# Ten of sixteen key and value weight tiles of two cross attentions computed in rounds 110 to 133 of a delta recurrence

## The chip, the cores and the metric

The kernel runs on one core of one Trainium2 chip. The metric is device time in microseconds of one execution. The core has five engines that run their own instruction streams in order and meet through semaphores: TensorE (PE, matmuls and transposes), VectorE (DVE), ScalarE (ACT), GpSimd (POOL) and SyncE (SP), which here only issues DMAs.

## The reference, cut to what matters

The reference runs two transformer blocks one after the other, on 512 tokens of width 1024. The first block's first layer has a gated delta recurrence, run over 512 latent and 256 context tokens in chunks, forward and backward, for 8 heads. The second block has two layers, and each of them holds a cross attention to a memory of 256 rows. The memory is an input, so its keys and values depend on nothing that the program computes:

```
for l in range(2):
    ...
    mem_n = rms_norm(mem, norm_mem[l])
    x = x + memory_cross_attention(rms_norm(x, norm_cross[l]), mem_n, xa_w_q[l], xa_w_kv[l], ...)

def memory_cross_attention(h, mem_n, w_q, w_kv, w_o, q_norm, k_norm):
    q  = rms_norm((h @ w_q).reshape(B, S, 4, 256), q_norm)
    kv = (mem_n @ w_kv).reshape(B, M, 2, 4, 256)      # w_kv is 1024 x 2048
    k, v = rms_norm(kv[:, :, 0], k_norm), kv[:, :, 1]
    ...softmax(q k / 16) v, then @ w_o
```

All is float32.

## The kernel before, in words

**Products.** A large product is done with three matmuls in the faster float32r type: every operand is cut into a high part (ACT copies it) and a low part (DVE subtracts the high part from the raw value), and `mm3` adds high x high, high x low and low x high (lines 259 to 261). Weights come in tiles of 1 MB, 128 partitions by 2048 values. SP loads them in the order in which PE takes them, into two raw slots; a load waits until the tile before it in its slot has been cut. The cut parts go to two places in `rw`, and a cut waits until the tile before last has been used. `tile` cuts one tile ahead; tiles marked `pieces` are cut in quarters by `split_quarter` at chosen rounds instead.

**The recurrence.** `rounds` (line 1744) runs 24 units (2 groups of 4 heads, 12 chunk visits each). A unit starts every 5 rounds and lives some 23 rounds, so up to five are alive, and there are 138 rounds. In each round every engine does its step of each unit alive, in program order, and then what `pe_between`, `act_between`, `dve_between` and `pool_between` (from line 2189 on) put behind it: dense projections of the first block (until about round 108), the ada rows (`SIDE_ROUNDS`, until round 114), and from round 104 the tails. A tail takes one finished group and chunk, norms it, turns it, gates it with Z (loaded from HBM by POOL) and writes the high and low parts into `H5` or `mT`, from where the output projection `dn_out` reads them. `TAILS` holds the round of each. The units' matmuls are float32, of 32, 64 or 128 columns. Bank sets: units have six PSUM banks, dense parts and tails two.

**The cross attentions.** `pe_cross` (line 3740) runs the output projection of the mixer before it (four weight tiles), turns the normed memory behind the second of them, and then makes keys and values: `pe_proj_tok` for four blocks of 512 columns, each of two weight tiles, for two groups of 128 memory rows. A tile is 24 matmuls of 512 columns. Keys are normed for each head (`act_key_norm`, `dve_key_norm`, lines 3840 and 3849) during the value tiles, turned, and then the query projection follows. POOL loads the raw memory and the gains in `pool_cross_loads` (line 3676).

Of the kernel before, what the change touches and what calls it, by code (L numbers as in the profile page):

```python
# [8 lines left out]
F32 = mybir.dt.float32  # L9
# [88 lines left out]
class Kernel:  # L98


    def __init__(self, nc, ctx, I, consts, out):
        self.nc, self.ctx, self.I, self.consts, self.out = nc, ctx, I, consts, out
        self.sems, self.book, self.freed, self.banks, self.tiles = {}, {}, {}, {}, []
        self.raw, self.pieces, self.slots, self.rws = set(), set(), [], []
        self.rehearsing = True
        self.arena = ctx.enter_context(nc.sbuf_tensor("arena", [128, A_END], F32))
        self.rx = ctx.enter_context(nc.sbuf_tensor("rx", [128, 12288], F32R))
        self.rw = ctx.enter_context(nc.sbuf_tensor("rw", [128, 8192], F32R))
        self.psum = ctx.enter_context(nc.psum_tensor("psum", [128, 4096], F32))
# [8 lines left out]
        self.g_s = nc.dram_tensor("g_s", [128, 4096], F32).ap()  # L118
        self.ident = self.mem(CO + C_ID, 128)
# [371 lines left out]
def r2(ap, a):  # L491
    return ap.rearrange("p (a n) -> p a n", a=a)
# [1574 lines left out]
def z_rounds(rnd, offset):  # L2067
# [109 lines left out]

def act_tail_hi(a, K, i, hg, c):
    a.wait_ge(*K.at("dn", len(STREAM) - 1, 1))
    a.wait_ge(*K.at("tail_z", hg, c))  # L2180
    a.cp(tail_toks(K, hg, c)[0], tail_z(K, i)).then_inc(*a.sig(("o_hi", hg, c)))

# [3 lines left out]
    v.lo(tail_toks(K, hg, c), tail_z(K, i)).then_inc(*v.sig(("o_lo", hg, c)))  # L2186


def pe_between(p, K, side, ms, rnd):

    for i, hg, c in tail_rounds(rnd, 3):
        pe_tail(p, K, i, hg, c, PART_BANKS)
    if rnd < 2:
        pe_part_post(p, K, DENSE - 2 + rnd, UNIT_BANKS)
    r = part_rounds(rnd, 9)
# [18 lines left out]


def act_between(a, K, side, ms, rnd):
    for i, hg, c in tail_rounds(rnd, 4):
        act_tail_hi(a, K, i, hg, c)
    if rnd < 2:
# [9 lines left out]
        act_G_rows(a, K, 1)  # L2229
    if rnd in SIDE_ROUNDS:  # L2230
        next(side, None)
    if rnd in TILE_ROUNDS:
        ms.append(a.skip())
    for q in {2: (0,), 4: (1,), 7: (2, 3)}.get(rnd - max([t for t in TILE_ROUNDS if t <= rnd]), ()):
        a.split_quarter(ms[-1], q)
    if rnd in (119, 122):
        a.ahead()
    if rnd == 84:
        act_tail_root(a, K, 0)
# [1500 lines left out]
def pe_cross(p, K, l, otag, W, ready, turn=None):  # L3740
# [98 lines left out]

def act_key_norm(a, K, l, t):  # L3840
    kt = cross_mem(K)[2]
    for j in range(2):
        a.wait_ge(*K.at(f"xk{l}{j}", "out", t))
# [37 lines left out]
def act_cross(a, K, l, otag):  # L3881
# [38 lines left out]
def dve_cross(v, K, l, otag):  # L3920
# [12 lines left out]
        if (t, h) == (3, 0):  # L3933
            dve_mem_lo(v, K, l)

    dve_out(v, K, otag, 8, 4, between={0: keys}, after=after, begun=l)
    for j in range(2):
        v.tile()
        v.tile()
        dve_tok_out(v, K, f"xk{l}{j}", range(2), lambda t: kt[:, t, j * 512:(j + 1) * 512])  # L3940
    for j in range(2):
        v.tile()
        v.tile()
        dve_key_norm(v, K, l, j)
        dve_tok_out(v, K, f"xv{l}{j}", range(2), lambda t: v_[:, t, j * 512:(j + 1) * 512])
# [1070 lines left out]
```

## Time and profile before

| what | value |
|---|---|
| median of 3 runs | 4089.51 us (4084.01 to 4093.94) |
| span of the profiled execution | 4093.5 us, 67946 instructions |
| PE busy | 3847.9 us, 94% |
| DVE, ACT, POOL busy | 2094.8, 1657.1 and 535.3 us |
| in_xa_w_kv loads | 16 of 1024 KB, landing 5.0 us after issue |
| k_s loads on POOL between 640 and 900 us | 8 of 256 KB, landing 3.4 us after issue |

The profile is one execution. Busy times don't count waiting. PEclk is the TensorE clock that was granted, as a share of 2.4 GHz. Line numbers are those of the kernel's file, and most instructions carry the line of a small helper, so places are found by time: the recurrence ends and `dn_out` begins at 828.9 us; the keys and values of the first cross attention are made from 2608 to 2653 us, those of the second from 3533 to 3578 us. The profile names a group by its line, its operands and its shape.

### The profile page before, as it was taken

What the parts mean: (1) busy time and instruction counts of PE and PEld (TensorE: products, weight loads), DVE (VectorE), ACT (ScalarE), POOL (GpSimd) and SP (SyncE); (2) the same over time, 40 slices, a digit from 0 to 9 for tenths busy, and PEclk for the clock granted to TensorE, in tenths of its full rate; (3) what the DMA queues carried; (4) which work ended last, traced back from release to release, by engine and by line L of the source; (5) the groups of instructions that cost most, each with busy time, mean ns of one, the idle gap of its engine ahead of it and who ended that gap; (6) DMA issues with size and microseconds to landing.
All of it is one profiled execution on the core that took longest, in us unless ns stands there. A gap on an engine that the chain in (4) does not pass through costs nothing.

```text
span 4093.5 us, 67946 instructions
## 1 busy us (share of the span) xinstructions
PE 3847.9 (94%) x28458; PEld 3180.3 (78%) x28458; DVE 2094.8 (51%) x3092; ACT 1657.1 (40%) x2695; POOL 535.3 (13%) x607
## 2 busy tenths in 40 slices
PE   6999999799999999988999889999999998999999
PEld 4888777678888877767887765778887877788887
DVE  3667755652212454565225644545665337645564
ACT  4445544322112343453223446444344346544333
POOL 0033444311200000020200000000210013000210
PEclk8999999799999999999999899999999999999999
DMA  5244554322221121122232310412332221312232
GB/s 164 82 140 148 171 165 146 99 88 62 78 67 52 63 82 38 42 79 87 93 98 96 70 52 1 136 53 83 103 100 93 93 93 36 124 53 83 93 103 83
DMA packets 238474, 367.71 MB, mean 90 GB/s; under 512 B 9859, under 2 KB 146774, under 8 KB 237910
## 3 DMA queue, kind: packets, MB, share of 16 engines
q1 hardware_dynamic: 219248, 300.49, 22.4%
q0 software_dynamic: 18368, 62.70, 5.2%
q8 instruction: 224, 3.67, 0.4%
q14 instruction: 84, 0.69, 0.1%
q10 hardware_dynamic: 550, 0.17, 0.0%
HBM read 344.36 MB, written 18.96 MB: 89 GB/s over the span
## 4 chain that ended last, share of the span: by engine, by line
PE 77%; DVE 12%; ACT 7%; issue 1%; DMA 1%; ACTq 0%; DVEq 0%; SPq 0%; POOL 0%; POOLq 0%
PE psum L259 21%; PE psum L260 20%; PE psum L261 20%; PE psum L256 14%; ACT arena L389 3%; DVE arena L289 3%; PE psum L265 2%; DVE arena L299 2%; DVE rw L289 2%; ACT rw L393 2%; ACT rx L393 1%; DVE rx L383 1%; DVE arena L303 1%; ACT arena L393 1%; DMA arena<-in_ada_w 1%
## 5 line engine op out<-in xcount | busy, mean ns | idle before, releaser
L259 PE MATMUL psum<-rx,rw 128*128 128x512 f32 (+2 forms) x2864 | 1049.5, 366 | 33.3 <-DVE rw L289 19.0
L260 PE MATMUL psum<-rx,rw 128*128 128x512 f32 (+2 forms) x2864 | 1023.1, 357 | 0.0
L261 PE MATMUL psum<-rx,rw 128*128 128x512 f32 (+2 forms) x2864 | 1021.9, 357 | 0.0
L289 DVE TENSOR_TENSOR rw<-arena,rw 128x2048 fp32r<-128x2048 f32 (+3 forms) x266 | 548.6, 2062 | 822.4 <-ACT rw L393 812.6
L256 PE MATMUL psum<-arena 32*32 32x32 f32 (+8 forms) x12982 | 759.8, 246 | 83.4 <-ACT arena L393 25.5
L256 PEld LDWEIGHTS psum<-arena 32*32 32x32 f32 (+4 forms) x12982 | 584.3, 133 | 217.0 <-issue 84.7
L393 ACT ACTIVATE rw<-arena 128x2048 fp32r<-128x2048 f32 (+3 forms) x266 | 453.6, 1705 | 707.3 <-PE psum L261 691.1
L259 PE MATMUL psum<-rw,rx 128*128 128x512 f32 (+1 forms) x1816 | 699.5, 385 | 26.5 <-DVE rx L383 13.6
L260 PE MATMUL psum<-rw,rx 128*128 128x512 f32 (+1 forms) x1816 | 689.3, 380 | 0.0
L261 PE MATMUL psum<-rw,rx 128*128 128x512 f32 (+1 forms) x1816 | 688.4, 379 | 0.0
L259 PEld LDWEIGHTS psum<-rx,rw 128*128 128x128 f32 (+1 forms) x2864 | 545.3, 190 | 163.5 <-issue 36.6
L261 PEld LDWEIGHTS psum<-rx,rw 128*128 128x128 f32 (+1 forms) x2864 | 545.1, 190 | 78.7
L260 PEld LDWEIGHTS psum<-rx,rw 128*128 128x128 f32 (+1 forms) x2864 | 546.2, 191 | 77.1 <-issue 3.3
L393 ACT ACTIVATE arena<-psum 128x512 f32<-128x512 f32 (+6 forms) x657 | 301.1, 458 | 660.1 <-PE psum L256 284.0
L454 POOL TENSOR_TENSOR arena<-arena 128x512 f32<-128x512 f32 (+4 forms) x228 | 355.6, 1560 | 1229.6 <-DVE arena L299 391.8
L259 PEld LDWEIGHTS psum<-rw,rx 128*128 128x128 f32 x1816 | 345.4, 190 | 106.0 <-DVE rx L383 25.8
L299 DVE SCALAR_TENSOR_TENSOR arena<-arena 128x512 f32<-128x512 f32 (+6 forms) x583 | 405.8, 696 | 35.7 <-ACT arena L389 13.7
L389 ACT ACTIVATE arena<-arena 128x512 f32<-128x512 f32 (+10 forms) x483 | 251.1, 520 | 393.4 <-DVE arena L299 185.4
L261 PEld LDWEIGHTS psum<-rw,rx 128*128 128x128 f32 x1816 | 345.5, 190 | 64.6
L260 PEld LDWEIGHTS psum<-rw,rx 128*128 128x128 f32 x1816 | 345.9, 190 | 60.6
L289 DVE TENSOR_TENSOR arena<-arena,psum 128x512 f32<-128x512 f32 (+3 forms) x308 | 151.8, 493 | 348.9 <-PE psum L261 201.7
L265 PE MATMUL psum<-arena 128*128 128x128 f32 (+3 forms) x1188 | 185.3, 298 | 91.9 <-DVE arena L289 26.1
(73 smaller groups left out, 2113.6 us busy)
## 6 DMA issues: line engine op xcount, KB each, us to landing
arena<-in_ffn_w_up SPq DMA_DIRECT2D x66, 1024.0 KB, 5.1
arena<-in_ada_w SPq DMA_DIRECT2D x48, 1024.0 KB, 6.5
arena<-in_ffn_w_down SPq DMA_DIRECT2D x40, 1024.0 KB, 5.0
arena<-in_ffn_w_gate SPq DMA_DIRECT2D x22, 1024.0 KB, 5.3
arena<-in_dn_w_in SPq DMA_DIRECT2D x16, 1024.0 KB, 5.9
arena<-in_xa_w_kv SPq DMA_DIRECT2D x16, 1024.0 KB, 5.0
arena<-in_hgrn_w_in SPq DMA_DIRECT2D x16, 1024.0 KB, 5.4
arena<-in_da_w_in SPq DMA_DIRECT2D x12, 1024.0 KB, 5.1
```

What stands on the lines that cost most here:

```text
L256: return self.e.matmul(out, l, r, start=start, stop=stop)
L259: self.e.matmul(out, l[0], r[0], start=start, stop=False)
L260: self.e.matmul(out, l[0], r[1], start=False, stop=False)
L261: return self.e.matmul(out, l[1], r[0], start=False, stop=stop)
L265: return self.e.transpose(out, a, self.K.ident[0:k, 0:k])
L289: return self.e.tensor_tensor(out, a, b, op)
L299: return self.e.scalar_tensor_tensor(out=out, in0=a, scalar=s, in1=b, op0=op0, op1=op1)
L303: return self.e.tensor_reduce(out, a, AX.X, op)
L383: return self.e.tensor_tensor(dst[1], src, dst[0].bitcast(F32), SUB)
L389: return self.e.activation(out, a, f, **kw)
L393: return self.e.activation(out, a, ACT.Copy, **kw)
L454: return self.e.tensor_tensor(out, a, b, op)
```

## The change

The memory is loaded once in round 70 into a new tensor `more`, its row norms are made in rounds 82 to 86, and it is turned and multiplied with the gain of each layer's memory norm in rounds 108 and 109 (first layer) and 124 and 125 (second). The turned rows go to blocks 0 and 3 of `H5`. Ten weight tiles (column blocks 0, 1, 2 of the first layer, 0 and 1 of the second) are used in rounds 110 to 133: each piece has 12 matmuls in its round and 12 in the next. The results go through `more` to a new HBM tensor `kv_s`, stored by POOL. In the cross attentions POOL loads them back; the keys, all of which come this way, are normed after the third tile of the output projection; three or two fewer column blocks are left in the loop. Tails of chunks 0 and 3 write to blocks 0 and 3 of `H5`, so two of them move from rounds 119 and 122 to 131 and 133; tails take unit banks now. The two early cuts of `dn_out` weights move from rounds 119 to 123 to rounds 134 to 137. The SBUF for `more` (12.4 KB of each partition) is taken from the scratch for descriptors of POOL's DMAs, set to 4096 bytes. An entry of `KV_PIECES` is a round, a layer, a column block, a half of the rows of the weights and a raw slot; `KV_TAKEN` holds the round in whose order SP loads each. DVE cuts a piece's tile one round ahead, ACT two, both in quarters. The edits of `dve_between` and `dve_cross` answer to those of ACT (its early cuts of `dn_out` move to rounds 135 and 137). The core of the diff:

```
-TAILS = ((104, 0, 5), (106, 0, 4), (110, 1, 5), (112, 0, 2), (114, 1, 4), (117, 0, 1), (119, 0, 3), (122, 0, 0), (125, 1, 2),
-         (129, 1, 1), (134, 1, 3), (139, 1, 0))
+TAILS = ((104, 0, 5), (106, 0, 4), (110, 1, 5), (112, 0, 2), (114, 1, 4), (117, 0, 1), (125, 1, 2), (129, 1, 1), (131, 0, 3),
+         (133, 0, 0), (134, 1, 3), (139, 1, 0))
+MEM_LOAD, MEM_SQUARE = 70, 82
+KV_TURN = (108, 124)
+KV_PIECES = ((110, 0, 0, 0, 0), (113, 0, 0, 1, 0), (116, 0, 1, 0, 1), (118, 0, 1, 1, 0), (120, 0, 2, 0, 1), (122, 0, 2, 1, 0),
+             (126, 1, 0, 0, 1), (128, 1, 0, 1, 0), (130, 1, 1, 0, 1), (132, 1, 1, 1, 0))
+KV_TAKEN = (94, 109, 112, 113, 115, 117, 119, 121, 126, 128)
...
+def pe_kv_step(p, K, m, t, l, j, kh):
+    key, w = ("kv", l, j, t), K.wview(m, 512, 4)
+    b = K.ps(*key) if kh else p.bank(*key, among=PART_BANKS[t:t + 1])
+    p.wait_ge(*K.at("lo", m))
+    for k in range(4):
+        if j == 0 and t == 0:
+            p.wait_ge(*K.at("kv_lo", l, kh * 4 + k))
+        ins = p.mm3(b[:, :], kv_toks(K, kh * 4 + k, t), [x[:, k, :] for x in w], kh + k == 0, kh * 4 + k == 7)
...
 def pe_between(p, K, side, ms, rnd):
+    for l, first in enumerate(KV_TURN):
+        if first <= rnd < first + 2:
+            for j in (2 * (rnd - first), 2 * (rnd - first) + 1):
+                pe_kv_turn(p, K, l, j)
     for i, hg, c in tail_rounds(rnd, 3):
-        pe_tail(p, K, i, hg, c, PART_BANKS)
+        pe_tail(p, K, i, hg, c, UNIT_BANKS)
...
+    for q, t, l, j, kh in kv_step(rnd, 0):
+        pe_kv_step(p, K, ms[KV_FIRST + q], t, l, j, kh)
  def act_between(a, K, side, ms, rnd):
...
+    for q, t, l, j, kh in kv_step(rnd, 1):
+        if kh:
+            act_kv_out(a, K, t, l, j)
+    for q, t, l, j, kh in kv_step(rnd, -2):
+        if t == 0:
+            for part in range(4):
+                a.split_quarter(ms[KV_FIRST + q], part)
...
-    if rnd in (119, 122):
+    if rnd in (134, 136):
         a.ahead()
...
 def act_tail_hi(a, K, i, hg, c):
+    if c in (0, 3):
+        a.wait_ge(*K.at("kv_used", *KV_PIECES[-1][1:3]))
...
 def pool_cross_loads(g, K, l):
+    if l:
+        g.wait_ge(*K.at("hgt_lo", 3))
+    pool_kv_load(g, K, l)
...
 def pe_cross(p, K, l, otag, W, ready, turn=None):
...
-    for j in range(2):
-        pe_proj_tok(p, K, f"xk{l}{j}", wkv[:, j * 512:(j + 1) * 512], K.mT, range(2), ("mem_lo", l))
-    for j in range(2):
-        pe_proj_tok(p, K, f"xv{l}{j}", wkv[:, 1024 + j * 512:1536 + j * 512], K.mT, range(2))
+    for j in KV_LEFT[l]:
+        pe_proj_tok(p, K, f"xkv{l}{j}", wkv[:, j * 512:(j + 1) * 512], K.mT, range(2), ("mem_lo", l))
...
 def act_cross(a, K, l, otag):
...
-    act_out(a, K, otag, 8, 4, between={0: lambda: act_mem_norm(a, K, l), 1: behind, 3: second}, begun=l)
+    def keys():
+        for t in range(2):
+            act_key_norm(a, K, l, t)
+
+    act_out(a, K, otag, 8, 4, between={0: lambda: act_mem_norm(a, K, l), 1: behind, 2: keys, 3: second}, begun=l)
...
-    nc = _bacc.Bacc("TRN2", target_bir_lowering=False, num_devices=1)
+    nc = _bacc.Bacc("TRN2", target_bir_lowering=False, num_devices=1, dynamic_dma_scratch_size=4096)
```

## Rows read from the trace of the kernel before

**Rows 1.** The page: busy time of PE, its 40 slices and the granted clock.

```profile
PE 3847.9 (94%) x28458; PEld 3180.3 (78%) x28458; DVE 2094.8 (51%) x3092; ACT 1657.1 (40%) x2695; POOL 535.3 (13%) x607
PE   6999999799999999988999889999999998999999
PEclk8999999799999999999999899999999999999999
```

**Rows 2.** Timeline of POOL: start, duration (us), instruction, idle before and its releaser.

```profile
651.27 0.54 POOL L227 DMA_DIRECT2D arena<-k_s  x1 [4.09 <-PE psum L256]
...
812.89 0.58 POOL L227 DMA_DIRECT2D arena<-k_s  x1 [7.10 <-ACT arena L393]
```

**Rows 3.** Busy time by stretch: length, PE, PEld, DVE, ACT, POOL, PEclk, DMA share, GB/s.

```profile
651.30:674.10 22.80, 21.91 (x438) 17.81 (x429) 11.24 (x26) 10.81 (x28) 9.40 (x15) 1.00 0.43 140
...
724.10:750.70 26.60, 20.38 (x406) 18.05 (x394) 15.55 (x39) 9.63 (x22) 9.94 (x16) 0.74 0.35 117
750.70:775.60 24.90, 16.55 (x396) 15.15 (x383) 19.47 (x34) 9.50 (x19) 8.25 (x13) 0.73 0.21 60
775.60:795.40 19.80, 13.76 (x344) 12.31 (x332) 13.91 (x25) 8.59 (x23) 8.70 (x11) 0.83 0.43 142
795.40:812.90 17.50, 12.53 (x165) 11.36 (x165) 11.26 (x27) 7.53 (x22) 5.86 (x10) 0.71 0.15 46
812.90:829.00 16.10, 10.23 (x59) 9.15 (x60) 8.49 (x16) 3.44 (x13) 6.31 (x6) 0.67 0.12 34
...
719.00:829.00 110.00, 78.55 (x1413) 70.75 (x1410) 70.37 (x140) 39.07 (x100) 39.06 (x53) 0.73 0.29 91
```

**Rows 4.** Waits of PE from 719 to 829 us: total, times, longest.

```profile
PE psum L265 <- DVE arena L289: 12.5, 7, 4.8
PE psum L256 <- DVE arena L289: 9.8, 7, 3.2
PE psum L256 <- ACT arena L393: 8.2, 5, 3.2
```

**Rows 5.** Timeline of ACT in the first cross attention: cuts of weight tiles.

```profile
2626.43 1.92 ACT L393 ACTIVATE rw<-arena 128x2048 fp32r<-128x2048 f32 x1 [3.52 <-PE psum L261]
2631.87 1.92 ACT L393 ACTIVATE rw<-arena 128x2048 fp32r<-128x2048 f32 x1 [2.17 <-PE psum L261]
```

**Rows 6.** Chain of waits: start, length (us), engine and line of each piece.

```profile
829.37 0.43 PE psum L260
...
2584.28 1.75 PE psum L265 x16
...
2645.16 0.23 PE psum L261
```

**Rows 7.** Busy time by stretch, at the end of the key and value tiles.

```profile
2650.00:2660.00 10.00, 8.25 (x59) 7.32 (x58) 8.09 (x12) 6.22 (x16) 0.00 (x0) 1.00 0.51 187
...
3570.00:3580.00 10.00, 8.24 (x38) 6.50 (x36) 6.79 (x8) 4.76 (x11) 0.00 (x0) 1.00 0.50 174
```

**Rows 8.** Chain of waits at the end of the first attention's tiles.

```profile
2654.76 0.50 DVE arena L299
2655.30 1.75 PE psum L265 x14
```

**Rows 9.** Timelines of ACT and DVE before the first attention's tiles.

```profile
2597.02 1.92 ACT L393 ACTIVATE rw<-arena 128x2048 fp32r<-128x2048 f32 x1 [4.54 <-PE psum L261]
...
2598.97 2.29 DVE L289 TENSOR_TENSOR rw<-arena,rw 128x2048 fp32r<-128x2048 f32 x1 [4.17 <-ACT rw L393]
...
2611.59 0.75 DVE L294 TENSOR_SCALAR arena<-arena 128x1024 f32<-128x1024 f32 x1
```

**Rows 10.** Quarter splits (300 to 700 us, min/median/max ns) and DVE's low parts (2586 to 2592).

```profile
L289 DVE TENSOR_TENSOR rw<-arena,rw x27: 691/693/1471, 302.9 to 646.4; 128x512 fp32r<-128x512 f32 x27
L393 ACT ACTIVATE rw<-arena x27: 629/632/634, 299.6 to 636.8; 128x512 fp32r<-128x512 f32 x27
L299 DVE SCALAR_TENSOR_TENSOR rx<-psum,arena,rx 128x256 fp32r<-128x256 f32 x8 | 3.9, 484 | 2.4 <-ACT rx L393 1.9
```

More of the change, by code:

```diff
@@ L108, in __init__ @@
         self.rw = ctx.enter_context(nc.sbuf_tensor("rw", [128, 8192], F32R))
+        self.more = ctx.enter_context(nc.sbuf_tensor("more", [128, 3104], F32))
         self.psum = ctx.enter_context(nc.psum_tensor("psum", [128, 4096], F32))
@@ L2186, in dve_tail_lo @@
     v.lo(tail_toks(K, hg, c), tail_z(K, i)).then_inc(*v.sig(("o_lo", hg, c)))
+MEM_LOAD, MEM_SQUARE = 70, 82
[3 more added lines that the diff above has]
+KV_TAKEN = (94, 109, 112, 113, 115, 117, 119, 121, 126, 128)
+KV_MOVED = tuple(tuple(j for q, i, j, kh, s in KV_PIECES if i == l and kh) for l in range(2))
@@ new lines, with kv_rows, kv_place, kv_cols @@
+KV_LEFT = tuple(tuple(j for j in range(4) if j not in moved) for moved in KV_MOVED)
+def kv_rows(K):
+    return K.more[:, 0:2048].rearrange("p (t n) -> p t n", n=1024)
+def kv_place(K, t):
+    return K.more[:, 2048 + t * 512:2560 + t * 512]
+def kv_cols(K):
+    return K.more[:, 3072:3104]
+def kv_toks(K, k, t):
+    c = 3 * t
+    return [x[:, k, c * 128:c * 128 + 128] for x in K.H5]
+def kv_feats(K, k):
+    return [x[:, k, :].rearrange("p (c n) -> p c n", n=128)[:, 0:4:3, :] for x in K.H5]
@@ new lines, in kv_step, with kv_before, pe_kv_turn @@
+def kv_step(rnd, offset):
+    return [(q, rnd - offset - x[0], *x[1:4]) for q, x in enumerate(KV_PIECES) if 0 <= rnd - offset - x[0] < 2]
+def kv_before(l, j):
+    done = [x[1:3] for x in KV_PIECES if x[3]]
+    i = done.index((l, j))
+    return done[i - 1] if i else None
+def pe_kv_turn(p, K, l, j):
+    for t in range(2):
+        p.wait_ge(*K.at("kv_row", t))
+    b = p.bank("kv_T", l, j, among=UNIT_BANKS)
+    for k in (2 * j, 2 * j + 1):
+        for t in range(2):
+            o = k % 2 * 256 + t * 128
+            ins = p.tr(b[:, o:o + 128], kv_rows(K)[:, t, k * 128:(k + 1) * 128])
+    ins.then_inc(*p.sig(("kv_T", l, j)))
+    p.close("kv_T", l, j)
@@ new lines, in pe_kv_step @@
+def pe_kv_step(p, K, m, t, l, j, kh):
[7 more added lines that the diff above has]
+    if kh:
+        ins.then_inc(*p.sig(key, ("used", m), ("kv_used", l, j)))
+        p.close(*key)
+    elif t:
+        ins.then_inc(*p.sig(("used", m)))
@@ new lines, in act_kv_out, with dve_kv_mean @@
+def act_kv_out(a, K, t, l, j):
+    if kv_before(l, j):
+        a.wait_ge(*K.at("kv_st", *kv_before(l, j), t))
+    a.wait_ge(*K.at("kv", l, j, t))
+    a.cp(kv_place(K, t), K.ps("kv", l, j, t)[:, :]).then_inc(*a.sig(("kv_out", l, j, t)))
+    a.free("kv", l, j, t)
+def dve_kv_mean(v, K):
+    for t in range(2):
+        c = kv_cols(K)
+        v.wait_ge(*K.at("kv_sq", t))
+        v.ts(c[:, 4 + t:5 + t], c[:, 2 * t:2 * t + 1], c[:, 2 * t + 1:2 * t + 2], 1e-6, ADD, ADD).then_inc(
+            *v.sig(("ms", "kv", t)))
@@ new lines, in pool_kv_store, with pool_kv_load @@
+def pool_kv_store(g, K, t, l, j):
+    g.wait_ge(*K.at("kv_out", l, j, t))
+    g.load(("kv_st", l, j, t), [(K.kv_s[l, j, t], kv_place(K, t))], f"kv_st{t}")
+def pool_kv_load(g, K, l):
+    kT, v_, kt, qt, qT = cross_mem(K)
+    for j in KV_MOVED[l]:
+        for t in range(2):
+            g.wait_ge(*K.at("kv_st", l, j, t))
+    g.load(("kv_ld", l), [((v_ if j >= 2 else kt)[:, t, j % 2 * 512:j % 2 * 512 + 512], K.kv_s[l, j, t])
+                          for j in KV_MOVED[l] for t in range(2)])
@@ L2203, in pe_between @@
         ms.append(p.take((0, part_weights(K, DENSE + 2 * len(ms))), slot=0, pieces=True))
+    for (q, l, j, kh, slot), taken in zip(KV_PIECES, KV_TAKEN):
+        if rnd == taken:
+            ms.append(p.take((0, K.I["xa_w_kv_2"][l][kh * 512:kh * 512 + 512, j * 512:j * 512 + 512]), slot=slot, pieces=True))
+    for q, t, l, j, kh in kv_step(rnd, 0):
+        pe_kv_step(p, K, ms[KV_FIRST + q], t, l, j, kh)
     if rnd < Z_FROM:
@@ L2216, in act_between @@
 def act_between(a, K, side, ms, rnd):
+    for l, first in enumerate(KV_TURN):
+        if first <= rnd < first + 2:
+            for j in (2 * (rnd - first), 2 * (rnd - first) + 1):
+                act_kv_hi(a, K, l, j)
     for i, hg, c in tail_rounds(rnd, 4):
@@ L2257, in dve_between @@
 def dve_between(v, K, side, ms, rnd):
+    for l, first in enumerate(KV_TURN):
+        if first <= rnd < first + 2:
+            for j in (2 * (rnd - first), 2 * (rnd - first) + 1):
+                dve_kv_lo(v, K, l, j)
     for i, hg, c in tail_rounds(rnd, 4):
@@ L2301, in pool_between @@
 def pool_between(g, K, side, rnd):
+    if rnd == MEM_LOAD:
+        g.load(("kv_mem",), [(kv_rows(K), K.I["mem_2"][0].rearrange("(t p) n -> p t n", p=128))])
+    for q, t, l, j, kh in kv_step(rnd, 2):
+        if kh:
+            pool_kv_store(g, K, t, l, j)
     if rnd in (1, 2):
@@ L3841, in act_key_norm @@
     kt = cross_mem(K)[2]
-    for j in range(2):
-        a.wait_ge(*K.at(f"xk{l}{j}", "out", t))
+    a.wait_ge(*K.at("kv_ld", l))
     for h in range(4):
@@ L3934, in after, with key_norms @@
             dve_mem_lo(v, K, l)
-    dve_out(v, K, otag, 8, 4, between={0: keys}, after=after, begun=l)
-    for j in range(2):
+    def key_norms():
+        for t in range(2):
+            dve_key_norm(v, K, l, t)
+    dve_out(v, K, otag, 8, 4, between={0: keys, 2: key_norms}, after=after, begun=l)
+    for j in KV_LEFT[l]:
         v.tile()
         v.tile()
[L3940 to L3945, printed above, removed]
+        dve_tok_out(v, K, f"xkv{l}{j}", range(2), lambda t: v_[:, t, j % 2 * 512:j % 2 * 512 + 512])
     for j in range(1, 4, 2):
```

64 lines of the change are left out of this document (52 added, 12 removed).

## The prediction

> **What bounds the kernel now.** I read the page from the top. TensorE is busy 94% of the span; of the 40 slices of part 2 the eighth (716 to 819 us) is the only one after the first in which PE falls to 7 tenths and the only one whose granted clock is as low as 7 tenths [rows 1]. So work taken out of a full stretch of PE is worth its whole time, and work put into the dip can be cheap. That dip is the second half of the delta recurrence. The loads of k_s on POOL are issued once per unit, that is once in five rounds, and date the rounds: 96 at 651.3 us, 101 at 674.1, 106 at 696.2, 111 at 724.1, 116 at 750.7, 121 at 775.6, 126 at 795.4, 131 at 812.9 [rows 2] (the first and the last of eight). The next view is the busy time in those stretches [rows 3]: rounds 96 to 100 have PE busy 21.9 of 22.8 us (96%) at clock 1.00; then the dense Z projections end, PE is busy 78.6 of 110 us from 719 to 829 and the mean granted clock is 0.73, between its levels of 1.2 and 2.4 GHz. Who ends PE's idle time there is in the waits [rows 4]: 30.5 us, on VectorE and ScalarE, no DMA. The rounds there are an alternation, PE for all units alive, then DVE and ACT.
>
> The other place is the keys and values of the two cross attentions. There PE is full. A tile's split on ACT comes each 5.44 us [rows 5]; 24 matmuls of 512 columns, one each 0.23 us [rows 6], make 5.5 us: the tiles go by PE's pace. Two holes stand at the end, where PE waits for the key norm of the last tile: 1.75 us in 2650 to 2660 and 1.76 us in 3570 to 3580 [rows 7], and the chain shows why (the last of four scales, and then the transposes [rows 8]).
>
> **The change: what goes.** Ten tiles leave the cross attentions (six of the first, four of the second): 10 x 5.44 = 54.4 us, all in a full PE. The two holes of the key norm go too, since all keys now come from HBM and are normed behind the third weight tile of the output projection: 3.5 us. Together 57.9. What is late next in their place? The x rows for the query projection: the last is scaled at 2611.59, before the second KV tile's split [rows 9], so the two tiles that stay in the first attention (11 us) still cover it. PE's wait for that split stays. The key norm costs DVE 4 us (8 scales of 0.50 [rows 8]) and ACT by estimate as much and half again (8 squares and two roots), 6 us, in a stretch where ACT sat idle 4.5 us and DVE 4.2 us [rows 9]; the next split slips by 1.5 us and PE wants it some 10 us later, so nothing; if that cover were gone, 1 to 2 us for each attention. The reloads (ten of 256 KB, behind loads that POOL issues anyway) have over 15 us before ACT wants them. Bounds for the saving: 50 (both norms and the fewer-tile cover late by 4 us each) to 59; I take 57.9.
>
> **What comes.** In rounds 110 to 133 PE gets 20 half steps of 12 matmuls: 240 x 0.23 = 55.2 us. 32 transposes turn the memory rows: 16 took 1.75 us at full clock [rows 6], so 3.5. Together 58.7 us. DVE gets 40 quarter splits of 0.69 (27.7 us) and 16 low parts of 0.48 (7.7); ACT 40 x 0.63 = 25.2, 16 high parts (by estimate like the low ones, 8) and ten copies of 512 columns (6) [rows 10]. POOL gets ten stores of about 0.55 us issue, SP's ten loads are the same ones, earlier. SP's order is one queue: the first load is put at round 94, and each later one waits for the split of the tile before it in its slot, with two rounds (some 10 us) for a transfer that lands in 5. The one that comes close is slot 1 at round 112, behind the last ada tile; its ACT split in round 114 has nothing that can wait for free, price 0 to 3 us once.
>
> Floor: PE work at full clock is 78.55 x 0.73 = 57.3 us from 719 to 829 [rows 3]; with 58.7 more it is 116 us in a stretch that took 110. So the rounds must grow by 6 us even if PE never waits, and a gain there is excluded. Ceiling: all in series, 58.7 + 27.7 + 7.7 = 94 us. In between by stretches of five rounds, PE busy times clock plus the new steps in them, over 0.92 (my choice between 0.96, which rounds 96 to 100 reach with DVE busy 49%, and 0.66, which rounds 116 to 120 have with DVE busy 78%; the new DVE share is near 75%, yet the filler is there for PE to do while DVE works):
> - rounds 106 to 110: one step, 16 transposes, 6.7 us of DVE: I take +3.
> - 111 to 115: 15.1 + 8.3 = 23.4, over 0.92 is 25.4, under the 26.6 that it takes, but DVE has 15.6 + 5.5 = 21; I take 28.6, +2.
> - 116 to 120: 12.1 + 13.8 = 25.9, 28.2 after 24.9: +3.3. DVE loses a whole split (2.3) and a tail here, and gains two tiles.
> - 121 to 125: 11.4 + 8.3 + 1.8 = 21.5, 23.4 after 19.8: +3.6.
> - 126 to 130: 8.9 + 13.8 = 22.7, 24.7 after 17.5: +7.2.
> - 131 to the end: PE has 6.9 + 8.3 + 0.9 = 16 in 16.1, but DVE has 8.5 and gets one tile (2.8), the two whole splits for dn_out (4.6) and two tails that had to wait for H5's blocks 0 and 3 (4.9): 20.8 in 16.1. I take 22: +6.
> The sum is +25. Everything queued behind a wait here is on the same in-order engines: behind PE's wait for a KV tile's low part stand that round's remaining projection and all of the next round's units. The tails now take a unit bank, so a unit's matmul can wait for the DVE gate: 0 to 1 us for each of 12, inside the 0.92. Before it, rounds 70 to 86 get a 1 MB load, four squares and two row scalings in a stretch like rounds 96 to 100, where ACT and DVE are half idle: 0 to 2, I take 0. The smaller DMA scratch I cost at nothing: POOL never waits on an issue in these rounds.
>
> 57.9 - 25 = 33 less. The profiled execution's span is 4093.5 us, 4 above the median of 4089.5 (0.1%); the same difference from the median gives 4056.
>
> **Two rules.** Rows: at 96% busy PE is granted 1.00; at 829 us, after a stretch in which it was busy 64%, matmuls of 512 columns come each 0.43 instead of 0.23 us, the lower level [rows 3, 6]. The Trainium skill, TensorE: Matmul & The Clock Gate, What's actually happening, says that throttled is the default and that activity releases it. By that rule the filler pays back part of its price in faster unit matmuls, as in the sum; were the clock to stay at 0.73, PE would need 78.6 + 80.4 = 159 us, +49.
> Row: of 27 quarter splits in the rounds before, one took 1.47 instead of 0.69 us [rows 10]. The skill speaks against the change here: SBUF — State Buffer, Who interferes with whom, has VectorE with two SBUF inputs and GpSimd's reads exclude each other. A split has two SBUF inputs. POOL is busy 39 of 110 us; if that share of 40 quarters took 0.78 more it is 11 us of DVE, and the sum would be +36 instead of +25, 4067.
>
> **Rivals.** (a) The rounds grow only by PE's floor, 6 us: for it, rounds 96 to 100 run nearly so, with the Z projections between; against, DVE had 48% there. 4037.5. (b) The clock does not come back, or DVE's collisions cost: +45 to +49, 4077 to 4081. Against it speaks clock 1.00 wherever PE is over 95% busy. (c) Slower: DVE and PE alternate, so each new step stands in series with its split. Price up to 94, 4126; it decides from a stretch of 58, that is from 2.9 us for each of the 20 half steps, more than the whole step of 2.76. For it: PE already waits 22 us for DVE there; against: PE's step is placed after the unit matmuls, just where it idles. (d) The change doesn't take from the cross attentions what it says, because keys or x rows come late there: 40 instead of 58, 4074. (e) POOL's transfers queue behind one another with the smaller scratch, so that k and v come a landing (3.4 us by the issues of the page) later in each of 6 units of these rounds: 20 more, 4076. Against it: the trace has no wait of POOL on an issue.
>
> **How the numbers follow.** Forecast 0.70, its own range 4042 to 4070; (a) 0.10; (b) 0.07; (c) 0.06; (d) 0.04; (e) 0.03. The range is 4036 (floor in full) to 4081 (clock not back). What a measurement can tell is about 0.2%, 8 us: faster 0.87, same 0.07 (upper ends of b and e, lower end of c), slower 0.06.
>
> **What would show it.** Right: the time from the k_s load of round 106 to the first dn_out matmul grows from 133 to about 158 us at a clock over 0.9; PE's busy share there near 87 to 92%; the KV stretches shrink from 44 us to 11 and 22, with no hole before the key transposes. Wrong: a stretch over 40, a clock under 0.85 from round 111, DVE rather than PE without idle time, or new holes at the KV tiles that stay or ahead of the output projection's last tile.

## The result, and the profile after

The changed kernel takes 4115.14 us (median, 4113.79 to 4122.67), the kernel before in the same session 4091.57 (4084.01 to 4093.94): ratio 1.0061, 95% interval 1.0046 to 1.0075. It is slower by some 24 us where 33 less was forecast, and it lies above the forecast range. The profiled spans say the same: 4114.2 against 4093.5.

The page of the profile says little about where. TensorE's busy time is what it was, to 0.1 us. Set against [rows 1], the slices show one difference: the dip, one slice wide before, is three wide (8, 7 and 8 tenths from 617 to 926 us). The clock in the last two of them is 8 tenths, where the one slice of before had 7:

```profile
PE 3847.8 (94%) x28490; PEld 3172.1 (77%) x28490; DVE 2106.8 (51%) x3139; ACT 1677.0 (41%) x2756; POOL 547.3 (13%) x628
...
PE   6999998789999998998899989999999998899999
...
PEclk8999999889999999999999999999999999999999
```

The dates of the rounds show it, as in [rows 2]. POOL's loads of k_s in the changed kernel (start, duration, instruction, idle before and its releaser), rounds 91 to 131:

```profile
631.86 0.54 POOL L229 DMA_DIRECT2D arena<-k_s  x1 [4.03 <-PE psum L258]
...
667.38 0.54 POOL L229 DMA_DIRECT2D arena<-k_s  x1 [17.80 <-PE psum L258]
...
690.14 0.54 POOL L229 DMA_DIRECT2D arena<-k_s  x1 [4.37 <-PE psum L258]
...
712.38 0.54 POOL L229 DMA_DIRECT2D arena<-k_s  x1 [4.35 <-PE psum L258]
...
757.30 0.54 POOL L229 DMA_DIRECT2D arena<-k_s  x1 [19.50 <-PE psum L258]
...
786.13 0.54 POOL L229 DMA_DIRECT2D arena<-k_s  x1 [4.32 <-PE psum L258]
...
822.26 0.54 POOL L229 DMA_DIRECT2D arena<-k_s  x1 [8.76 <-PE psum L258]
...
851.11 0.55 POOL L229 DMA_DIRECT2D arena<-k_s  x1 [8.06 <-ACT arena L395]
...
881.99 0.54 POOL L229 DMA_DIRECT2D arena<-k_s  x1 [10.43 <-ACT arena L395]
```

Put beside the loads of before, the five-round stretches are, in us:

| rounds | before | after | growth | forecast |
|---|---|---|---|---|
| 91 to 95 | 21.8 | 35.5 | +13.7 | 0 |
| 96 to 105 | 44.9 | 45.0 | +0.1 | 0 |
| 106 to 110 | 27.9 | 44.9 | +17.0 | +3 |
| 111 to 115 | 26.6 | 28.8 | +2.2 | +2 |
| 116 to 120 | 24.9 | 36.2 | +11.3 | +3.3 |
| 121 to 125 | 19.8 | 28.8 | +9.0 | +3.6 |
| 126 to 130 | 17.5 | 30.9 | +13.4 | +7.2 |
| 131 to dn_out | 15.7 | 28.5 | +12.7 | +6 |

With 2.4 us that the profile lost before round 91, dn_out's first matmul comes 81.8 us later (910.4 for 828.6) where 25 was forecast. From there the two kernels run in parallel until the first cross attention, as SP's loads show. (Start, duration, queue entry. The first fence is the kernel before, the second the changed one; the first cross attention lies between the second entry of each and the third, the second one behind the fourth.)

```profile
1239.70 183.66 SPq L470 DMA_DIRECT2D arena<-in_ffn_w_down  x12
...
2247.55 127.61 SPq L470 DMA_DIRECT2D arena<-in_ab_w_in  x10
...
2677.43 73.59 SPq L470 DMA_DIRECT2D arena<-in_xa_w_o  x4
...
3323.04 163.19 SPq L470 DMA_DIRECT2D arena<-in_hgrn_w_out  x4
```

```profile
1320.11 182.35 SPq L472 DMA_DIRECT2D arena<-in_ffn_w_down  x12
...
2325.23 127.67 SPq L472 DMA_DIRECT2D arena<-in_ab_w_in  x10
...
2720.23 73.60 SPq L472 DMA_DIRECT2D arena<-in_xa_w_o  x4
...
3366.20 163.66 SPq L472 DMA_DIRECT2D arena<-in_hgrn_w_out  x4
```

The lag is 80.4, 77.7, then 42.8 and 43.2, and 20.7 at the end: the first attention gave 34.9 us, the second 22.5, together 57.4 where 57.9 was forecast. So the saving came about as forecast, and the error is in the recurrence. The 57.4 is the difference of two single executions, in which the lag drifts by 4 us (81.8 to 77.7) where the code is the same. Taken from the profiles of all the kernels below that have the change, the time from dn_out to the end is 45 to 61 us shorter than in the profile of before.

There are two kinds of growth. In rounds 91 to 95 and 106 to 110 a single wait makes most of it. Waits of PE from 600 to 925 us (total, times, longest), and below them the two places in PE's timeline:

```profile
PE psum L258 <- DMA arena<-in_ada_w: 25.2, 4, 12.9
PE psum L267 <- DVE arena L291: 17.6, 7, 4.3
PE psum L258 <- ACT arena L395: 9.2, 7, 3.3
PE psum L261 <- DVE rw L291: 5.9, 3, 2.3
```

```profile
659.81 1.94 PE L258 MATMUL psum<-arena 128*32 128x512 f32 x8 [11.71 <-DMA arena<-in_ada_w]
...
748.18 1.94 PE L258 MATMUL psum<-arena 128*32 128x512 f32 x8 [12.92 <-DMA arena<-in_ada_w]
```

PE waits for tiles of the ada rows, which the change does not touch. SP's timeline says why; the kernel before first, then the changed one:

```profile
601.50 118.07 SPq L470 DMA_DIRECT2D arena<-in_ada_w  x11
719.61 65.13 SPq L470 DMA_DIRECT2D arena<-in_dn_w_out  x4
```

```profile
603.89 23.85 SPq L472 DMA_DIRECT2D arena<-in_ada_w  x3
649.63 0.37 SPq L472 DMA_DIRECT2D arena<-in_xa_w_kv  x1
650.04 58.22 SPq L472 DMA_DIRECT2D arena<-in_ada_w  x6
740.25 0.37 SPq L472 DMA_DIRECT2D arena<-in_xa_w_kv  x1
740.66 9.87 SPq L472 DMA_DIRECT2D arena<-in_ada_w  x2
```

SP stood from 627.7 (603.89 + 23.85) to 649.6 at the load of the first piece, since the tile before it in its slot was not cut yet. SP's waits from 620 to 655 us and from 700 to 745 us (total, times, longest) name DVE's cut as what released it both times:

```profile
SPq L472 <- DVE rw L291: 21.9, 1, 21.9
...
SPq L472 <- DVE rw L291: 32.0, 1, 32.0
```

The next ada tile was issued 0.4 us behind the first piece's load, and PE, after 11.7 us without work, could go on at 659.8. The same happened at the second piece: SP stood from 708.3 to 740.25, and PE waited 12.9 us. The Trainium skill, DMA: Bandwidth & Descriptors, Anatomy of one DMA, says that a semaphore wait of a transfer happens on the issuing sequencer and not on the DMA engines; by that rule everything behind a waiting load is held though the DMA engines could take it, and the trace agrees: the ada tile went out only behind the load that waited, and the DMA engines' busy share in rounds 91 to 95 is 0.41, below the 0.47 of before.

The other kind is from round 111 on. Busy time by stretch (length; PE, PEld, DVE, ACT, POOL; PEclk, DMA share, GB/s): rounds 91 to 95 and 111 to dn_out of before, then 91 to 95, 106 to 110 and 111 to dn_out of after.

```profile
629.40:651.30 21.90, 21.90 (x454) 18.15 (x440) 14.38 (x29) 11.69 (x29) 9.83 (x15) 1.00 0.47 150
...
724.10:827.40 103.30, 71.85 (x1327) 64.59 (x1315) 68.29 (x136) 38.67 (x98) 39.06 (x53) 0.74 0.27 85
```

```profile
631.90:667.40 35.50, 23.79 (x442) 19.19 (x434) 14.28 (x29) 11.69 (x29) 9.88 (x15) 0.81 0.41 136
...
712.40:757.30 44.90, 27.78 (x462) 22.08 (x452) 21.56 (x44) 16.77 (x34) 9.11 (x15) 0.77 0.38 127
...
757.30:909.20 151.90, 121.18 (x1570) 100.73 (x1558) 95.44 (x177) 70.56 (x151) 44.16 (x63) 0.89 0.37 124
```

The last row of each is worth a small sum. The stretch is PE's idle time (length minus busy), plus PE's work as if at full clock (busy times PEclk), plus what the clock took (the rest of busy):

| kernel | length | PE idle | work at full clock | lost to the clock |
|---|---|---|---|---|
| before | 103.3 | 31.5 | 53.2 | 18.7 |
| after | 151.9 | 30.7 | 107.9 | 13.3 |

The work grew by 54.7 us, as the forecast has it (55.2 of matmuls and transposes), and the clock gave 5.4 of it back. But PE's idle time, into which the new work was meant to go, is still all there. DVE is busy 27.2 us more in the stretch and ACT 31.9. That suggests that the new work of these two made as much new idle time of PE as the new matmuls filled; e3, e4 and e12 below test it.

### The profile page after: what moved, and what is told of

Its sections match the earlier page's. It is cut to its first block, busy times and chain, and to the rows that moved or that the text cites. A ratio compares the mean times of both kernels' runs of the same rounds, so it can differ in the third digit from the quotient of the medians.

```text
span 4114.2 us, 68180 instructions
## 1 busy us (share of the span) xinstructions
PE 3847.8 (94%) x28490; PEld 3172.1 (77%) x28490; DVE 2106.8 (51%) x3139; ACT 1677.0 (41%) x2756; POOL 547.3 (13%) x628
## 4 chain that ended last, share of the span: by engine, by line
PE 76%; DVE 13%; ACT 8%; DMA 2%; issue 2%; ACTq 0%; DVEq 0%; SPq 0%
PE psum L261 21%; PE psum L262 20%; PE psum L263 20%; PE psum L258 13%; ACT arena L391 3%; DVE arena L291 3%; DVE rw L291 3%; PE psum L267 2%; DVE arena L301 2%; ACT rw L395 2%; ACT rx L395 1%; DMA arena<-in_ada_w 1%; DVE arena L305 1%; ACT arena L395 1%; DVE rx L385 1%
## 5 line engine op out<-in xcount | busy, mean ns | idle before, releaser
L261 PE MATMUL psum<-rx,rw 128*128 128x512 f32 (+2 forms) x2864 | 1051.7, 367 | 32.4 <-DVE rw L291 18.1
L291 DVE TENSOR_TENSOR rw<-arena,rw 128x2048 fp32r<-128x2048 f32 (+3 forms) x296 | 557.8, 1884 | 790.5 <-ACT rw L395 777.9
L258 PE MATMUL psum<-arena 32*32 32x32 f32 (+8 forms) x12982 | 746.2, 245 | 95.7 <-DMA arena<-in_ada_w 41.5
L258 PEld LDWEIGHTS psum<-arena 32*32 32x32 f32 (+4 forms) x12982 | 569.4, 131 | 230.7 <-issue 99.0
L261 PE MATMUL psum<-rw,rx 128*128 128x512 f32 (+1 forms) x1816 | 704.9, 388 | 33.4 <-DVE rw L291 16.3
L261 PEld LDWEIGHTS psum<-rx,rw 128*128 128x128 f32 (+1 forms) x2864 | 546.5, 191 | 165.3 <-issue 38.7
L262 PEld LDWEIGHTS psum<-rx,rw 128*128 128x128 f32 (+1 forms) x2864 | 547.6, 191 | 77.4 <-issue 3.3
L261 PEld LDWEIGHTS psum<-rw,rx 128*128 128x128 f32 x1816 | 347.4, 191 | 115.5 <-DVE rx L385 25.9
L291 DVE TENSOR_TENSOR arena<-arena,psum 128x512 f32<-128x512 f32 (+3 forms) x308 | 151.9, 493 | 370.2 <-PE psum L263 195.5
L267 PE MATMUL psum<-arena 128*128 128x128 f32 (+3 forms) x1188 | 181.4, 293 | 93.7 <-DVE arena L291 30.7
```

Source lines behind the costliest of these rows:

```text
L258: return self.e.matmul(out, l, r, start=start, stop=stop)
L261: self.e.matmul(out, l[0], r[0], start=start, stop=False)
L262: self.e.matmul(out, l[0], r[1], start=False, stop=False)
L267: return self.e.transpose(out, a, self.K.ident[0:k, 0:k])
L291: return self.e.tensor_tensor(out, a, b, op)
```

## The experiments

All ratios are to the kernel before, run on the same chip. A profile is one execution, and outside the changed rounds executions scatter: round 96 begins between 645 and 659 us in the experiments below, and from dn_out to the end the profiles show 3205 to 3221 us. The stretches repeat better where the code is the same: from round 111 on e1 and e11 differ by 0.1 us, e8 and e9 by less than 0.1, e10 and e13 by 2.0. So single runs are read by stretch, not by total. The kernels:

| kernel | time | ratio (95%) | round 96 to dn_out | 111 to dn_out |
|---|---|---|---|---|
| before | 4089.5 | | 176.1 | 103.3 |
| after | 4115.1 | 1.0061 (1.0046 to 1.0075) | 241.8 | 151.9 |
| e1_order | 4097.35 | 1.0020 (1.0011 to 1.0029) | 239.9 | 153.7 |
| e2_scratch | 4089.76 | 1.0003 (0.9992 to 1.0014) | | |
| e3_no_matmuls | 4095.5, one run | | 220.7 | 137.4 |
| e4_no_splits | 4075.3, one run | | 209.5 | 126.3 |
| e12_neither | 4062.3, one run | | 192.8 | 111.7 |
| e5_front | 4095.86 | 1.0014 (1.0003 to 1.0024) | 237.7 | 150.2 |
| e6_back | 4096.13 | 1.0011 (1.0000 to 1.0022) | 238.7 | 151.1 |
| e8_whole | 4087.58 | 0.9992 (0.9979 to 1.0005) | 224.5 | 137.1 |
| e10_whole_only | 4087.53 | 0.9994 (0.9984 to 1.0003) | 222.8 | 137.8 |
| e11_early_only | 4097.04 | 1.0012 (1.0003 to 1.0021) | 232.0 | 153.8 |
| e9_early | 4074.87 | 0.9963 (0.9947 to 0.9978) | 214.5 | 137.1 |
| e13_early_whole | 4079.37 | 0.9961 (0.9947 to 0.9975) | 215.7 | 139.8 |

(The kernel before had medians of 4089.5 to 4091.6 over these sessions, so kernels of different sessions are compared by their ratios: one thousandth is 4.1 us. In the two last columns dn_out is dated by the tail transposes just ahead of it, 1.2 us before its first matmul. Of after, 91 to 95 with its 13.7 us lies ahead of the column. e3, e4 and e12 leave out work that the keys and values need, so only their times count.)

**The queue (e1_order).** Only the places of two loads in SP's order change:

```
-KV_TAKEN = (94, 109, 112, 113, 115, 117, 119, 121, 126, 128)
+KV_TAKEN = (96, 111, 112, 113, 115, 117, 119, 121, 126, 128)
```

> The changed kernel with the loads of the first two pieces' tiles put two rounds later in SP's order (rounds 96 and 111 instead of 94 and 109), so that each stands behind an ada tile that PE wants at once instead of ahead of it. Theory (SP's queue): in the changed kernel the load of a piece waits for the cut before it in its slot, and the ada tile behind it in the queue reaches PE 11.7 and 12.9 us late; both waits vanish, rounds 91 to 96 go from 35.5 to about 22 us and 106 to 111 from 44.9 to about 31, and the kernel is 25 to 31 us faster than the changed one: 4084 to 4090, the same as before within 0.2%. Rival (the ada tiles are late because the rounds there are short of DMA bandwidth or of ACT and DVE): the waits move but stay, gain under 8 us.

Measured: 17.8 us less than after (4097.35 for 4115.14; 16.8 by the ratios), more than the rival's 8 but below the 25 to 31 expected. Rounds 91 to 95 are back at 21.8, 106 to 110 at 36.2 from 44.9 (31 was expected), but 96 to 100 grew from 22.8 to 27.8: the ada tile of round 97 now stands behind the first piece's load, and PE waits 3.9 us for it. In the waits of PE (600 to 910 us) the line of 25.2 us is down to

```profile
PE psum L258 <- DMA arena<-in_ada_w: 4.2, 2, 3.9
```

So the queue made this wait, and two numbers in a list were worth 17 us.

**The scratch (e2_scratch).** The kernel before with one argument more:

```
-    nc = _bacc.Bacc("TRN2", target_bir_lowering=False, num_devices=1)
+    nc = _bacc.Bacc("TRN2", target_bir_lowering=False, num_devices=1, dynamic_dma_scratch_size=4096)
```

> The kernel before with 4096 bytes of scratch for POOL's DMA descriptors, nothing else. Theory: no transfer of POOL waits for it, within 0.2% of before (4084 to 4098). Rival: POOL's transfers queue, k and v come late in the recurrence, 15 us or more slower.

No difference: 1.0003. Rival (e) is out.

**Matmuls or cuts (e3_no_matmuls, e4_no_splits, e12_neither).** On top of e1, e3 leaves out 180 of the 240 matmuls, e4 three of four quarter cuts on both engines, e12 both:

```
     for k in range(4):
+        if k != 3 * kh:
+            continue
```

```
-            for part in range(4):
+            for part in range(3, 4):
```

> As e1_order, but of the 12 matmuls of each of the 20 half steps only 3 are done (the keys and values are left incomplete); cuts, copies, stores and waits stay. It leaves out 180 matmuls of 0.23 us, 41 us at full clock. Theory (PE's added work mostly fills holes only in part, order of the streams costs the rest): rounds 111 to the first dn_out matmul, 153.5 us in the changed kernel and 104.8 before, fall by 15 to 30 us, not by 41, and stay 20 to 35 over before. Rival (PE's work is the bound): they fall by 41 or more. Rival (the cuts on ACT and DVE are the bound): they fall by less than 10.

> As e1_order, but of the four quarter cuts of each of the ten pieces only one is done on ACT and on DVE (three quarters of the operands are stale, so keys and values are wrong); all matmuls stay. It leaves out 30 x 0.78 = 23 us on DVE and 30 x 0.65 = 20 us on ACT. Theory (the cuts stand ahead of the units' and tails' steps in the order of ACT and DVE): rounds 111 to the first dn_out matmul fall by 12 to 25 us. Rival (PE's added matmuls alone stretch the rounds): by less than 5.

> e1 with one of four matmul groups of each half step (60 of 240 matmuls) and one of four quarter cuts of each tile: leaves three quarters of both out. Theory (chain of cuts and matmuls in series, e3 gave 16 us and e4 27 us): if the two add, 154 - 43 = 111 us from round 111 to dn_out, near the 103 to 105 of the kernel before, total about 4060. Rival (the rest of the growth is neither: turned tails, tails in unit banks, copies, the later whole cuts for dn_out): 120 us or more stays with both gone, total 4068 or more.

From round 111 to dn_out, in the order e1, e3, e4, e12 (columns as above):

```profile
736.30:890.00 153.70, 123.15 (x1567) 102.39 (x1559) 95.23 (x177) 70.73 (x151) 44.33 (x63) 0.88 0.36 123
```

```profile
735.10:872.50 137.40, 89.07 (x1397) 74.79 (x1387) 96.51 (x177) 70.70 (x151) 43.29 (x63) 0.78 0.41 139
```

```profile
733.70:860.00 126.30, 111.69 (x1573) 93.32 (x1560) 73.51 (x150) 53.49 (x124) 44.34 (x63) 0.96 0.44 149
```

```profile
740.10:851.80 111.70, 84.31 (x1398) 71.33 (x1387) 74.89 (x150) 53.46 (x124) 43.33 (x63) 0.84 0.51 174
```

Against e1's 153.7, e3 is 16.3 less, e4 27.4 less, e12 42.0 less; 16.3 and 27.4 add to 43.7, so the two costs add nearly as if neither hid the other. e3 lies at the low end of what was expected, e4 above it, and e12 came as expected (111). Each of the three is one run. By the same sum as above: e3 has 38.9 us of full-clock work less than e1 (69.5 for 108.4), but PE's idle time goes up from 30.6 to 48.3, and the clock from 0.88 down to 0.78. e4 keeps the work (107.2) and has idle time 14.6 and clock 0.96. So the matmuls that e3 lacks filled 17.7 us of PE's idle time, and the cuts that e4 lacks made 16.0: this bears the reading above out. The cuts are the dearer half: 21.7 us of DVE and 17.2 of ACT, 27 quarters on each, were worth 27.4 us, and 38.9 us of PE's work 16.3. Of the +50.4 that e1 has over before, 8.4 stay in e12: a quarter of both kinds of work, the low parts, the copies, the moved tails and dn_out's late cuts. I did not separate those.

**The order (e5_front, e6_back).** e5 puts PE's piece ahead of the round's tail transposes; e6 puts the cuts last in the round on ACT and DVE:

```
+    for q, t, l, j, kh in kv_step(rnd, 0):
+        pe_kv_step(p, K, ms[KV_FIRST + q], t, l, j, kh)
     for i, hg, c in tail_rounds(rnd, 3):
         pe_tail(p, K, i, hg, c, UNIT_BANKS)
...
-    for q, t, l, j, kh in kv_step(rnd, 0):
-        pe_kv_step(p, K, ms[KV_FIRST + q], t, l, j, kh)
```

```
-    for q, t, l, j, kh in kv_step(rnd, -2):
-        if t == 0:
-            for part in range(4):
-                a.split_quarter(ms[KV_FIRST + q], part)
...
         r = z_rounds(rnd, 4 + 2 * s)
         if r is not None:
             act_part_raw(a, K, r, s)
+    for q, t, l, j, kh in kv_step(rnd, -2):
+        if t == 0:
+            for part in range(4):
+                a.split_quarter(ms[KV_FIRST + q], part)
...
```

> As e1_order, and on PE a piece's 12 matmuls come ahead of the tail's transposes in a round, not behind them. In e1_order PE waits 17.3 us for DVE ahead of the tails' transposes, seven times, with the piece's matmuls ready behind them. Theory (order of PE's stream costs a part): these waits fall to under 8 us and the kernel gets 5 to 12 us faster than e1_order (4097), to 4085 to 4092. Rival (the cuts on DVE and ACT set the pace, PE's order doesn't matter): less than 3 us.

> As e1_order, and on ACT and DVE the cuts of a piece's tile stand at the end of their round, behind the tail's norm, gate and squares. Theory (the cuts delay the tails' and units' steps that stand behind them on their engine): PE's waits for DVE ahead of the tails (17.3 us) fall by half or more, 6 to 15 us faster than e1_order. Rival (it is the amount of the cuts, 31 us on DVE, that costs, wherever in the round they stand): less than 4 us, with the waits only moved to the units' steps.

Both came out 1 to 2 us under e1 in the medians (2 to 4 by the ratios), and 3.5 and 2.6 us shorter from round 111 to dn_out. That is what the rivals said, not the 5 to 15 us of the theories. The idle time moved instead: in e5 the waits of PE's transposes for DVE (L267) fell from 17.3 to 8.3 us and its waits for a piece's low part (L261) rose from 8.0 to 16.4; in e6 they are 10.6 and 12.9.

**Fewer instructions for the same cut (e8_whole, e10_whole_only).** e10 is e1 with each tile cut in one instruction on each engine; e8 has the orders of e5 and e6 as well. The edit of e10:

```
-            for part in range(4):
-                a.split_quarter(ms[KV_FIRST + q], part)
+            a.tile_hi(ms[KV_FIRST + q])
...
-            for part in range(4):
-                v.split_quarter(ms[KV_FIRST + q], part)
+            v.tile_lo(ms[KV_FIRST + q])
```

> As e1_order with both orders changed (pieces' matmuls first on PE, cuts last on ACT and DVE), and each piece's tile cut in one instruction of 2048 columns on ACT and DVE instead of four of 512. A whole cut took 2.29 on DVE and 1.92 on ACT, four quarters 3.1 and 2.6 in this stage: 8 us less on DVE, 7 on ACT. Theory (the cuts and their place are what stretches the rounds): rounds 111 to dn_out, 153.7 us in e1_order, fall by 15 to 30; 4070 to 4083. Rival (the depth of the chain PE, DVE, ACT in a round sets the pace): less than 8 us from e1_order.

> The loads placed as in e1 (rounds 96 and 111) and the orders of the change on PE, ACT and DVE; only the ten tiles are cut whole (one ACT instruction of 1.92 us for four of 0.65, one of DVE of 2.29 us for four of 0.78) instead of in quarters. Theory (the fixed cost of the four pieces is a cost by itself): ACT saves 7 us and DVE 8.4 us, and since the work is in series with PE in these rounds about half or more of the 15 us returns: 107 to 111 from round 111 to dn_out down from 154 to 142 to 147 us, total 4085 to 4091. Rival (the gain of e8 needs the order, because a whole cut placed in front of the conversions holds the units longer in one go): 150 us or more, total 4095 or more.

111 to dn_out falls by 15.9 us in e10 and 16.6 in e8: the whole cuts do it and the order adds nothing that can be seen. In medians it is 9.8 us each (10.6 and 11.5 by the ratios). The stretch of e10 is shorter than the 142 to 147 expected and its total is as expected; e8's stretch is as expected and its total is above the 4083. DVE's cuts from 712 to 900 us in the changed kernel (first) and in e10 (second; two of its twelve are cuts for dn_out), as count, busy, mean ns and idle before:

```profile
L291 DVE TENSOR_TENSOR rw<-arena,rw 128x512 fp32r<-128x512 f32 x40 | 31.3, 783 | 3.0
```

```profile
L291 DVE TENSOR_TENSOR rw<-arena,rw 128x2048 fp32r<-128x2048 f32 x12 | 27.9, 2328 | 0.8
```

Four quarters are 4 x 783 = 3.13 us, a whole cut 2.33; on ACT 4 x 0.631 = 2.52 against 1.91. That is 1.4 us for a tile. The means hold some cuts that took much longer than the median: in the changed kernel the four quarters from 881.63 us took 5.49 us, beside two instructions of POOL in the same time. At the medians (0.692 and 2.292) DVE's part is 0.48 us for a tile and not 0.80. The stretch has 12.3 us less of DVE and ACT than in e1 (6.6 and 5.7) and is 15.9 shorter. By the sum above 6.9 of that is idle time of PE (30.6 to 23.7) and 7.9 is the clock, which is granted at 0.94 for 0.88. From 111 to dn_out in e10:

```profile
740.70:878.50 137.80, 114.13 (x1569) 95.28 (x1559) 88.61 (x150) 65.03 (x124) 47.68 (x63) 0.94 0.41 137
```

The Trainium skill, VectorE: DVE Perf Modes, The TRN2 errata, says that operations reading SBUF pay a fixed cost for each instruction on VectorE and ScalarE; by that rule three instructions less on each engine save time for the same elements, and the trace agrees (2.33 for 3.13 us on DVE, 1.91 for 2.52 on ACT).

**The load early enough (e11_early_only, e9_early, e13_early_whole).** The first two pieces are loaded in rounds 101 and 106 and the first is cut in 102 and 103, so that a cut frees the slot soon after. e11 does it on e1, e9 on e8, e13 on e10:

```
-KV_TAKEN = (96, 111, 112, 113, 115, 117, 119, 121, 126, 128)
+KV_HI = (102, 111, 114, 116, 118, 120, 124, 126, 128, 130)
+KV_LO = (103, 112, 115, 117, 119, 121, 125, 127, 129, 131)
+KV_TAKEN = (101, 106, 112, 113, 115, 117, 119, 121, 126, 128)
...
-    for q, t, l, j, kh in kv_step(rnd, -2):
-        if t == 0:
+    for q, at in enumerate(KV_HI):
+        if rnd == at:
```

> e1 with the first two pieces' loads issued in rounds 101 and 106 and the first one cut in rounds 102 and 103; quarters and the orders of the change stay, save that cuts are listed by round. Theory (SP's one queue: with a cut soon after each load, no ada tile stands behind a waiting load): PE's waits for ada tiles fall from 4.2 to under 1 us, rounds 96 to 100 return to 23 us, the time from round 111 to dn_out stays at 153 us, and the total is 4084 to 4087 (e1 minus 11 to 13, as from e8 to e9). Rival (the gain from e8 to e9 came from something that needs whole cuts): total 4092 or more.

> As e8_whole, and the first piece's tile is loaded behind the ada tile of round 100 and cut in rounds 102 and 103, where DVE is half idle, the second is loaded behind that of round 105; so no load ahead of an ada tile has to wait for a cut. e1_order still shows PE waiting 3.9 us for an ada tile at round 97 and 36.2 us for rounds 106 to 110 (27.9 before). Theory (SP's queue and the cuts): 6 to 13 us faster than e8_whole, rounds 96 to 101 back to 22.8 us, 106 to 111 under 33. Rival (the rest there is PE's new work, 1.8 us of transposes and 2.8 of matmuls, and DVE's low parts): less than 4 us.

> The loads and cut rounds of e11 (first two pieces loaded in rounds 101 and 106) with whole cuts as in e10, and the order of the change on every engine: e9 without its orders. Theory (two independent costs, the queue and the number of instructions of a cut; the order on PE, ACT and DVE is worth nothing): round 96 to dn_out takes 214 to 217 us as in e9 (214.5), and the total lies at 4075 to 4081. Rival (the order matters once the cuts are whole, since the first tile's whole cut in rounds 102 and 103 stands ahead of the conversions in a stretch where PE is full): 219 us or more from round 96 to dn_out, total 4083 or more.

By stretches, rounds 96 to 110 go from 86.2 us in e1 to 78.2 in e11, from 87.4 in e8 to 77.4 in e9, and from 85.0 in e10 to 75.9 in e13; PE's waits for ada tiles are 1.0 us or less. By medians e9 is 12.7 under e8 and e13 8.2 under e10, by the ratios 11.9 and 13.5. But e11 is only 0.3 under e1 (3.3 by the ratios), where 11 to 13 was expected and the rival had said 4092 or more: its profile shows the 8 us inside the stretch and loses them again outside it, within the scatter named above. The two intervals (1.0011 to 1.0029 and 1.0003 to 1.0021), taken as independent, allow a gain of up to 9 us. Whether e11's missing gain is scatter stays open; the other two pairs show the gain. e13 met its own forecast on both counts (215.7 and 4079.4), so the orders of e9 are worth nothing that can be told. e9 came as expected too (6 to 13 under e8).

e9 and e13 beat both kernels, the one before by 0.4%. Their recurrence is 38 to 40 us longer than before from round 96 on, for some 57 saved in the attentions. In e13 rounds 106 to 110 take 30.9 us, 3.0 more than before, which is the forecast's figure for them.

## Why the prediction was wrong, point by point

- *Ten tiles and two holes, 57.9.* Right as far as it can be read: 57.4 by the lags of this pair of profiles, 45 to 61 over all of them.
- *Scratch at nothing, key norms covered, reloads in time.* Right: e2 for the scratch. PE's wait of 1.8 us ahead of the key transposes is gone in both attentions; its wait for a tile's low part there is 1.6 us for 1.9 in the first and 2.8 for 1.6 in the second.
- *PE's added work, 58.7.* Right: 54.7 of full-clock work from round 111 on, and one half step and the first 16 transposes before it.
- *"SP's order is one queue … The one that comes close is slot 1 at round 112 … price 0 to 3 us once".* This is the step that failed first. I looked at each piece's load and asked whether it comes in time for its own cut. I never asked who stands behind it: the ada tiles, a tile for each of PE's side rounds, which SP issued before as one entry of eleven with no other load between them, from 601.5 us. Two loads put ahead of their slot's cut held the queue for 22 and 32 us. The two stretches were forecast at +3 and measured +30.7. Of that, PE's waits for ada tiles are 25.2 us, and the mean granted clock of rounds 91 to 95 is 0.81 for 1.00; 17.8 back in e1, and by stretches 8 to 10 more with the loads and the first cut placed as in e9, e11 and e13.
- *"PE busy times clock plus the new steps, over 0.92".* The second failure. Full-clock work over length in 111 to dn_out is 107.9 / 151.9 = 0.71, after 0.52 in the kernel before (53.2 / 103.3); PE's busy share is 80% there and 76% from round 106 on, where 87 to 92 was forecast. One part of the slip is in the bounds: the sum divides busy times clock by 0.92, but the 0.66 of rounds 116 to 120, which I took as the lower bound, is the busy share alone; with their clock of 0.73 it is 0.49 [rows 3]. I chose 0.92 because the filler stands where PE idles. That is nearer to what the matmuls do without the cuts: in e4, with a quarter of the cuts, the ratio is 107.2 / 126.3 = 0.85. With their cuts the pieces bring 3.1 us of DVE and 2.5 of ACT for 5.5 of PE, on the two engines that PE was waiting for [rows 4]. DVE itself was busy only 63% of the stretch, so neither engine was the bound by itself: PE and DVE waited in turn. The terms from round 111 on were sized at 22.1 together and measured 48.6. Of these 26.5 us, e10 gets 15.9 back by whole cuts alone.
- *40 quarters at 0.69.* They took 0.78 in the mean (31.3 us for 27.7). The rule on VectorE and GpSimd in the prediction put 11 us there; the row shows 3.6. The longest four lie beside work of POOL, but no run takes POOL's work away, so the cause isn't shown.
- *The clock at over 0.9.* 0.89 from 111 on (0.74 before), so the clock did come back with the filler, as the rule on it in the prediction has it, and e3 without most of the filler is at 0.78. Rival (b) is not what happened. But what came back was 5.4 us, since PE still stood idle for 30.7.
- *Rival (c), slower by alternation in series.* Nearest to what came. Its mechanism held in part: 48.6 us from round 111 on, short of the 58 from which it decides; with the queue's share the growth was 81.8. I gave it 6 in 100 because PE's step is placed after the unit matmuls; e5 and e6 show that the place is worth little, 1 to 4 us.

## What to carry to other kernels

When a load is inserted into an engine's in-order DMA queue, price it by what is behind it: take the time at which its slot comes free, and see which transfer of the old order would then be late. Idle time of an engine is a cheap place for new work only as far as the engines that end the idle time get little of it. Add up what each filler step asks of those engines, in its own instruction sizes, and count it in series until a row shows otherwise: here 38.9 us of cuts (DVE and ACT together) cost 27.4 us, and 38.9 us of matmuls 16.3. And cut tiles whole where no wait asks for quarters.

## What was not expected of the hardware

Leaving out 38.9 us of TensorE's full-clock work shortened the stretch by only 16.3 us (e3), since the clock fell from 0.88 to 0.78 and the idle time grew by 17.7. Taking 12.3 us of work off DVE and ACT shortened it by 15.9, more than the work itself, since half of the gain was TensorE's clock (e10).
